# Two block ends, eight feed-forward edges: one norm folded into the next, and VectorE and ScalarE work put in another order

## The chip, the cores and the metric

The kernel runs on one core of a Trainium2 chip. The metric is the device time of one execution in microseconds (us); lower is better. The engines are TensorE (PE in the rows; its weight loads are PEld), VectorE (DVE), ScalarE (ACT), GpSimd (POOL) and SyncE (SP), which issues the weight DMAs.

## The reference

Batch 1, 256 tokens, width 1024, in float32. A first block of two hybrid attention layers ends in an RMS norm; its output is the input of a second block, in which each of two layers is a feed-forward, a mixer (recurrent, then spatial) and a feed-forward again.

```python
def rms_norm(x, w):                      # rms_norm_2 is the same, with NORM_EPS = 1e-6 = EPS
    xf = x.astype(jnp.float32)
    y = xf * lax.rsqrt(jnp.mean(xf * xf, axis=-1, keepdims=True) + EPS)
    return (y * w.astype(jnp.float32)).astype(x.dtype)

def swiglu(x, w_in, w_out):              # w_in: 1024 x 5632, w_out: 2816 x 1024
    g, u = jnp.split(x @ w_in, 2, axis=-1)
    return (jax.nn.silu(g) * u) @ w_out

    x = x + gate_x * merge_branches(...)          # end of a hybrid layer; @ w_out is its last product
...
    return rms_norm(x, final_norm_w)              # end of the first block

    for i in range(DEPTH):                        # second block, DEPTH = 2
        h = h + 0.5 * swiglu(rms_norm_2(h, ffn1_norm[i]), ffn1_w_in[i], ffn1_w_out[i])
        hn = rms_norm_2(h, mix_norm[i])
        h = h + m                                 # m: mixer of hn
        h = h + 0.5 * swiglu(rms_norm_2(h, ffn2_norm[i]), ffn2_w_in[i], ffn2_w_out[i])
    return rms_norm_2(h, final_norm)
```

Between the first block and the second two norms follow each other: with x the output of the last hybrid layer, the feed-forward reads rms_norm_2(rms_norm(x, final_norm_w), ffn1_norm[0]), and the residual goes on from rms_norm(x, final_norm_w).

## The kernel before

**Layout.** Activations lie with the model's 1024 columns on partitions, as 8 chunks (KC) of 128, and tokens along the row: `x[:, k, 0:256]` is chunk k. The weights are 516 tiles of 128x1024 floats. SyncE brings them in order into a ring of 6 (`raw`). Each float32 weight is multiplied as two float32r parts: ScalarE copies a tile to `w_hi` (L1626, ring of 4), VectorE subtracts to get `w_lo` (L1924). Both are the step `split(t)`. Activations are split likewise: `h_hi` by ScalarE (L1642), `h_low` by VectorE (L2019). Here the step is called `split_x`.

**A feed-forward** has FC = 22 hidden chunks i and three weight tiles for each: g (gate), u (up) and o (down), in the order g0 u0 g1 u1 o0 g2 u2 o1 ... g21 u21 o20 o21. A g or u tile is 8 chunk products of two matmuls each (L2490 over 512 columns, `h_hi` and `h_low` side by side, and L2492), an o tile is 8 output chunks of three matmuls (L2482 to L2484). The gate lands in PSUM bank G[i % 2] and the up product in S[i % 2]; the downs gather in four output banks, M among them after the norm is through with it. For each i VectorE sums the two halves of the gate (L2289), multiplies by `rstd` (L2292), ScalarE takes Silu (L1780), GpSimd multiplies by `rstd` again (L1552, for the up half of the product), VectorE sums the up half (L2305) and multiplies (L2308), ScalarE makes `hid_hi` (L1785) and VectorE `hid_lo` (L2313); the down of i needs both. The last chunk's up product is taken in one piece, so it has no sum (L2303 instead of L2305 and L2308). The feed-forward's code on each engine is a hand-written order: two rounds by hand at the start, a loop over four rounds at a time (ROUND), and four rounds and the tail by hand. AHEAD = 3: in round i the splits of the tiles five to seven places on stand between the steps of round i.

**The norm is late.** A feed-forward multiplies un-normed chunks (x times the norm's weight) and puts the root in afterwards, since it is a factor per token. The squares (ScalarE L1636) are added (VectorE L1935) and summed over partitions on TensorE (`norm_mean`, L2598), VectorE adds EPS (L2012), GpSimd takes the power -0.5 (L1517), TensorE spreads it over the partitions (`norm_spread`, L2638) and VectorE copies it to `rstd` (L2004). `norm_mean` stands behind u0 and `norm_spread` within g1, at chunk 5. Before the second block only one norm isn't late: the last hybrid layer's ("residual"), which the next norm's squares need. It stands between the blocks with matmuls on constants to fill the time (`keep_busy`, L2542), and scales x itself (L2056).

**The order.** `build_schedule` makes one list of steps, and each engine runs its part of it in that order; `add_after_split` puts a step behind the next split. `bank_residuals` is the list behind a feed-forward (and behind the recurrent mixer): per output bank a residual (L2356) and the splits of its two chunks, then one weight split and the squares that are left (`late_squares`).

**Waits.** A step waits for counters of other engines. A weight split of tile n on ScalarE waits until TensorE has used tile n - 4; TensorE's first product of a tile waits for its `w_lo`.

## Time and profile before

| | us |
|---|---|
| median of 3 runs | 1994.42 (1992.77 to 1996.35) |
| the profiled execution | 1993.69, of which its span is 1992.0 |
| TensorE busy | 1952.9 (98%) |
| VectorE busy | 1220.5 (61%) |
| ScalarE busy | 894.3 (45%) |
| GpSimd busy | 227.9 (11%) |

The blocks meet at 1038 us. The feed-forwards begin their first tile at about 1044, 1323, 1514 and 1791 us and their last down ends at about 1237, 1514, 1706 and 1979 us. The recurrent mixer lies between the first and the second, the spatial one between the third and the fourth; the third follows the second directly. Matmuls overlap in the pipeline: a row gives a matmul's start and how long it was under way, and what counts for the time is the distance from start to start. Where TensorE waited, a row ends in the idle time in brackets, counted from the end of the matmul before. The idle time is thus less than what the wait cost.

### The profile page before, as it was taken

The numbers are of one execution on the slowest core, as the hardware profiler recorded it, in microseconds if no ns is written. First come the engines' busy times: TensorE is split into PE (matmuls) and PEld (weight loads), VectorE is DVE, ScalarE is ACT, GpSimd is POOL, SyncE is SP. The second block draws the span as 40 slices with busy tenths as digits, with TensorE's granted clock in tenths as the row PEclk, the third lists the DMA queues.
The fourth block names the chain that finished last, engine by engine and source line by source line (L and its number), as shares of the span: only waits on it lengthen the run. The fifth ranks groups of instructions, "written<-read, shape, count | busy, mean of one in ns | idle before, by whom it ended". The sixth has DMA issues, their size and how long they took to land. (4 is left out here: it accounts for less than half of the span.)

```text
span 1992.0 us, 35392 instructions
## 1 busy us (share of the span) xinstructions
PE 1952.9 (98%) x13247; PEld 1703.2 (86%) x13247; DVE 1220.5 (61%) x1962; ACT 894.3 (45%) x1426; POOL 227.9 (11%) x241
## 2 busy tenths in 40 slices
PE   8999999999999999999999999999999999999998
PEld 6777887777787788998998999989998999998997
DVE  6554443355443655546557777887777777676775
ACT  5444232244332544335545444764445444554443
POOL 1000100111122001211121000000001000201000
PEclk9999999999999999999999999999999999999999
DMA  8221443411234323343355555445555555445553
GB/s 317 82 72 64 144 145 128 145 62 58 80 103 151 111 93 104 109 142 114 129 169 166 184 188 170 150 156 184 188 190 183 188 189 188 151 157 172 190 186 109
DMA packets 79429, 289.23 MB, mean 145 GB/s; under 512 B 8912, under 2 KB 9168, under 8 KB 79312
## 3 DMA queue, kind: packets, MB, share of 16 engines
q1 hardware_dynamic: 77616, 281.61, 42.4%
q0 software_dynamic: 1120, 4.72, 0.8%
q8 instruction: 85, 1.39, 0.3%
q10 hardware_dynamic: 576, 1.24, 0.2%
q14 instruction: 32, 0.26, 0.1%
HBM read 286.49 MB, written 1.05 MB: 144 GB/s over the span
## 5 line engine op out<-in xcount | busy, mean ns | idle before, releaser
L1924 DVE TENSOR_TENSOR w_lo<-raw,w_hi 128x1024 fp32r<-128x1024 f32 x484 | 598.5, 1241 | 313.2 <-ACT w_hi L1626 312.3
L1626 ACT ACTIVATE w_hi<-raw 128x1024 fp32r<-128x1024 f32 x484 | 508.0, 1055 | 407.9 <-PE bank L2484 247.6
L2490 PE MATMUL bank<-h,w_hi 128*128 128x512 f32 x1376 | 487.6, 396 | 4.0 <-DVE h L2019 3.4
L2482 PE MATMUL bank<-h,w_hi 128*128 128x512 f32 (+1 forms) x1344 | 473.3, 352 | 3.6 <-issue 1.7
L2484 PE MATMUL bank<-h,w_lo 128*128 128x512 f32 (+1 forms) x1344 | 453.1, 337 | 0.0
L2483 PE MATMUL bank<-h,w_hi 128*128 128x512 f32 (+1 forms) x1344 | 452.2, 336 | 0.0
L2492 PE MATMUL bank<-h,w_lo 128*128 128x256 f32 x1376 | 385.6, 280 | 0.0
L2490 PEld LDWEIGHTS bank<-h,w_hi 128*128 128x128 f32 x1376 | 258.1, 188 | 62.8 <-DVE h L2019 4.5
L2482 PEld LDWEIGHTS bank<-h,w_hi 128*128 128x128 f32 x1344 | 254.2, 189 | 53.8 <-issue 28.2
L2484 PEld LDWEIGHTS bank<-h,w_lo 128*128 128x128 f32 x1344 | 254.2, 189 | 28.3
L2483 PEld LDWEIGHTS bank<-h,w_hi 128*128 128x128 f32 x1344 | 254.7, 190 | 24.5 <-issue 1.9
L2492 PEld LDWEIGHTS bank<-h,w_lo 128*128 128x128 f32 x1376 | 259.9, 189 | 0.0
L2482 PE MATMUL bank<-hid_hi,w_hi 128*128 128x256 f32 x704 | 198.0, 281 | 8.5 <-DVE hid_lo L2313 8.4
L2483 PE MATMUL bank<-hid_lo,w_hi 128*128 128x256 f32 x704 | 197.1, 280 | 0.0
L2484 PE MATMUL bank<-hid_hi,w_lo 128*128 128x256 f32 x704 | 196.9, 280 | 0.0
L2482 PEld LDWEIGHTS bank<-hid_hi,w_hi 128*128 128x128 f32 x704 | 132.3, 188 | 13.7 <-DVE w_lo L1924 6.0
L1552 POOL TENSOR_TENSOR silu_g<-silu_g,rstd 128x256 f32<-128x256 f32 x88 | 65.6, 745 | 631.5 <-ACT silu_g L1780 631.5
L1780 ACT ACTIVATE silu_g<-silu_g 128x256 f32<-128x256 f32 x88 | 36.9, 419 | 215.2 <-DVE silu_g L2292 215.2
L2483 PEld LDWEIGHTS bank<-hid_lo,w_hi 128*128 128x128 f32 x704 | 132.5, 188 | 0.0
L2484 PEld LDWEIGHTS bank<-hid_hi,w_lo 128*128 128x128 f32 x704 | 132.3, 188 | 0.0
L1717 ACT ACTIVATE work<-bank,row_stat 128x512 f32<-128x512 f32 (+1 forms) x96 | 58.4, 613 | 67.8 <-DVE row_stat L2175 67.8
L2175 DVE TENSOR_REDUCE row_stat<-bank 128x1 f32<-128x512 f32 (+1 forms) x96 | 53.0, 593 | 33.8 <-PE bank L2670 33.8
(242 smaller groups left out, 2383.4 us busy)
## 6 DMA issues: line engine op xcount, KB each, us to landing
raw<-in_weights SPq DMA_DIRECT2D x516, 512.0 KB, 3.4
early<-in_first SPq DMA_DIRECT2D x10, 512.0 KB, 13.2
bias<-in_rpb POOLq DMA_DIRECT2D x8, 384.0 KB, 3.4
early_o<-in_first SPq DMA_DIRECT2D x4, 512.0 KB, 16.3
x<-in_tokens SPq DMA_DIRECT2D x2, 512.0 KB, 6.0
x<-in_tokens ACTq DMA_DIRECT2D x2, 512.0 KB, 8.4
work<-in_first SPq DMA_DIRECT2D x2, 512.0 KB, 16.4
out<-cols_out SPq DMA_DIRECT2D x4, 256.0 KB, 2.6
```

What stands on the lines that cost most here:

```text
L1552: pool.tensor_tensor(v, v, rstd[:, 0:SEQ], ALU.mult).then_inc(silu_scaled, 1)
L1626: nc.scalar.activation(w_hi[:, n % SPLIT, :], raw[:, t % RAW, :], ACT.Copy).then_inc(hi_ready, 1)
L1717: nc.scalar.activation(probs[:, hp, 0:u.keys], S[use % 2][:, 0:u.keys], ACT.Exp, bias=row_stat[:, 0, i:i + 1], accum_out=row_stat[:, 1, i: ...
L1780: nc.scalar.activation(silu_g[:, i % 2, :], silu_g[:, i % 2, :], ACT.Silu).then_inc(silu_ready, 1)
L1924: dve.tensor_tensor(w_lo[:, t % RAW, :], raw[:, t % RAW, :], w_hi[:, SPLIT_NO[t] % SPLIT, :].bitcast(F32), ALU.subtract).then_inc(lo_ready, 1)
L2175: dve.tensor_reduce(row_stat[:, 0, i:i + 1], s[:, 0:u.keys], AX_X, ALU.max, negate=True)\
L2482: nc.tensor.matmul(dst, w_hi[:, SPLIT_NO[t] % SPLIT, at], hi, start=start, stop=False, skip_group_check=shared)
L2483: nc.tensor.matmul(dst, w_hi[:, SPLIT_NO[t] % SPLIT, at], lo, start=False, stop=False, skip_group_check=shared)
L2484: return nc.tensor.matmul(dst, w_lo[:, t % RAW, at], hi, start=False, stop=stop, skip_group_check=shared)
L2490: nc.tensor.matmul(bank[:, :], w_hi[:, SPLIT_NO[t] % SPLIT, at], h[:, k, 0:BOTH], start=k == 0, stop=k == KC - 1, skip_group_check=True)
L2492: return nc.tensor.matmul(bank[:, 0:SEQ], w_lo[:, t % RAW, at], h_hi[:, k, 0:SEQ], start=False, stop=k == KC - 1, skip_group_check=True)
```

## The change

**Blocks' end.** The norm between the blocks is no step of its own any more. The last hybrid layer's products go on as before, and behind each of them the chunk is split at once with `fold_w` = final_norm_w * ffn1_norm[0], and squared. TensorE sums squares with two columns, w/D and w*w/D (`fold_cols`), behind the products 3 to 7 of `w_out`, and the last three within the feed-forward's `norm_mean`. From the two means VectorE makes two sums in two dependent operations, GpSimd takes four roots instead of two, `norm_spread` spreads 512 columns instead of 256: the root of both norms together in `rstd[:, 0:256]` and the first norm's own in `rstd[:, 256:512]`. The residual x is scaled by the latter in the first feed-forward's last four rounds (`renorm`, 8 operations on VectorE), and `bank_residual` waits for it. The two steps of filling matmuls (26 in the trace) go.

**Start of each feed-forward.** VectorE sums gate 0, takes the mean, splits tile t0+3, sums up 0, copies `rstd`, scales gate 0, scales up 0 by `rstd` itself and multiplies; then it splits t0+4. GpSimd has no part in chunk 0. In round 0 `hid` and `low` stand ahead of the next split.

**End of each feed-forward.** VectorE's last product and `low` stand ahead of the split a+3. On TensorE five output chunks of o20 stand ahead of o21's instead of four.

**Behind a feed-forward and the recurrent mixer.** The late squares stand ahead of the weight split instead of behind it.

```diff
@@ schedule_layer
+    if layer:
+        s.add("fold_weights")
+        norm = new_norm(s, live, "h", "fold", "fold")
+        jobs = s.product_pair(("w_out", "w_out"), n=live, src="m")
+        for dc in range(KC):
+            job = jobs[dc] if dc < 2 else s.product("w_out", n=live, src="m", norm=None)
+            up = s.add("gated_residual", job=job, dc=dc, layer=layer, cols=live)
+            add = s.add if dc == KC - 1 else s.add_after_split
+            norm.chunks.append(add("split_x", norm=norm, k=dc, up=up, h=s.count("h")))
+            square(s, norm, dc, 1, up, after_split=dc < KC - 1)
+            if dc >= 3:
+                norm_part(s, norm, dc - 3)
+        return norm
@@ build_schedule
-    norm.how, norm.layer = "residual", ("final_norm_w", 0)
-    s.flush()
-    norm_mean(s, norm)
-    s.keep_busy(5, "G")
-    norm_spread(s, norm)
-    s.keep_busy(8, "G")
-    before, norm = norm, new_norm(s, SEQ, "h", ("ffn1_norm", 0), "dve")
-    for q in range(KC // 2):
-        ups = [normed(s, before, k) for k in (2 * q, 2 * q + 1)]
-        follow(s, norm, q, [None] * (2 * q) + ups)
-    late_squares(s, norm)
@@ bank_residuals
+    late_squares(s, after)
     if s.tile < NT:
         s.add("split", t=s.tile + AHEAD - 1)
-    late_squares(s, after)
@@ vector: norm_mean_step, norm_spread_step
+                if norm.add_n == "fold":
+                    dve.wait_ge(m_full, norm.m + 1)
+                    dve.wait_ge(rstd_rows, norm.rows)
+                    means = M[:, 0:4].rearrange("p (b two) -> p two b", two=2)
+                    dve.tensor_scalar(row_mean[:, 2:4], means[:, 0, :], EPS, None, ALU.add).then_inc(fold_mean, 1)
+                    dve.wait_ge(fold_mean, 1)
+                    dve.scalar_tensor_tensor(out=row_mean[:, 0:2], in0=row_mean[:, 2:4], scalar=EPS,
+                                             in1=means[:, 1, :], op0=ALU.mult, op1=ALU.add).then_inc(m_free, 1)
+                    return
...
+                if norm.add_n == "fold":
+                    dve.tensor_copy(rstd[:, :], M[:, :]).then_inc(m_free, 1)
+                    return
@@ vector: renorm, and the steps of the first chunk in ffn_step
+            def renorm(k, norm):
+
+                at = PARAM_AT["final_norm_w"] + k
+                dve.scalar_tensor_tensor(out=x[:, k, 0:SEQ], in0=x[:, k, 0:SEQ], scalar=par[:, at:at + 1],
+                                         in1=rstd[:, SEQ:BOTH], op0=ALU.mult, op1=ALU.mult).then_inc(renormed, 1)
...
+                def first_mult():
+                    dve.wait_ge(up_summed, UP_SUMS * f + 1)
+                    dve.tensor_tensor(hidden[:, 0, :], hidden[:, 0, :], rstd[:, 0:SEQ], ALU.mult).then_inc(up_scaled, 1)
+                    dve.wait_ge(up_scaled, f + 1)
+                    dve.wait_ge(silu_ready, FC * f + 1)
+                    dve.tensor_tensor(hidden[:, 0, :], hidden[:, 0, :], silu_g[:, 0, :], ALU.mult).then_inc(hid_ready, 1)
...
                 def round_(i, r=None):
                     a = t0 + AHEAD + 3 * i
-                    split(a + 2, r)
-                    low(i, r)
+                    if i == 0:
+                        low(0)
+                        split(a + 2)
+                    else:
+                        split(a + 2, r)
+                        low(i, r)
...
                     else:
                         gate(i + 1)
-                        split(a + 3)
                         mult(i + 1)
                         low(i + 1)
+                        split(a + 3)
                         split(a + 4)
 
+                gate_sum(0)
+                norm_mean_step(st)
                 split(t0 + AHEAD)
-                split(t0 + AHEAD + 1)
-                norm_mean_step(st)
+                first_up_sum()
                 norm_spread_step(st)
                 dve.wait_ge(m_free, st.norm.m_spread + 1)
-                gate(0)
-                mult(0)
+                gate_scale(0)
+                first_mult()
+                split(t0 + AHEAD + 1)
                 round_(0)
...
                 for i in range(FC - 1 - peeled, FC - 1):
+                    if st.norm.add_n == "fold":
+                        for k in range(2):
+                            renorm(2 * (i - (FC - 1 - peeled)) + k, st.norm)
                     round_(i)
@@ tensor: last_downs
-                    down(FC - 2, dcs=range(4), done=False)
+                    down(FC - 2, dcs=range(5), done=False)
                     down(FC - 1, dcs=range(4), done=False)
-                    for dc in range(4, KC, 2):
-                        down(FC - 2, dcs=(dc, dc + 1), first=False, done=dc == KC - 2)
-                        down(FC - 1, dcs=(dc, dc + 1), first=False, done=dc == KC - 2)
+                    down(FC - 2, dcs=(5,), first=False, done=False)
+                    down(FC - 1, dcs=(4, 5), first=False, done=False)
+                    down(FC - 2, dcs=(6, 7), first=False)
+                    down(FC - 1, dcs=(6, 7), first=False)
```

How the instructions stand is shown for three places. The first is TensorE where the blocks meet; `m_hi` is the last hybrid layer's input of `w_out`, `h` the feed-forward's. Before:

```order
L2484 MATMUL bank<-m_hi,w_lo 128x256
L2598 MATMUL bank<-con,scaled 128x1 x2
L2598 MATMUL bank<-con,square 128x1 x2
L2542 MATMUL bank<-con 128x128 x5
L2638 MATMUL bank<-con,stats 128x128 x2
L2542 MATMUL bank<-con 128x128 x8
L2490 MATMUL bank<-h,w_hi 128x512
```

After:

```order
L2561 MATMUL bank<-m_lo,w_hi 128x256
L2562 MATMUL bank<-m_hi,w_lo 128x256
L2675 MATMUL bank<-fold_cols,square 128x2 x2
L2568 MATMUL bank<-h,w_hi 128x512
L2570 MATMUL bank<-h,w_lo 128x256
```

Of the mean, the filling matmuls and the spread nothing is left between the blocks but one pair of sums; each such matmul is two records in the trace.

The second is VectorE from the second feed-forward's last chunk to the third's first. Before, from the last gate's scaling on:

```order
L2292 TENSOR_TENSOR silu_g<-silu_g,rstd 128x256
L1924 TENSOR_TENSOR w_lo<-raw,w_hi 128x1024
L2303 TENSOR_TENSOR hidden<-silu_g,bank 128x256
L2313 TENSOR_TENSOR hid_lo<-hidden,hid_hi 128x256
L1924 TENSOR_TENSOR w_lo<-raw,w_hi 128x1024
L2356 SCALAR_TENSOR_TENSOR x<-bank,x 128x2x256 x2
```

After:

```order
L2341 TENSOR_TENSOR silu_g<-silu_g,rstd 128x256
L2352 TENSOR_TENSOR hidden<-silu_g,bank 128x256
L2379 TENSOR_TENSOR hid_lo<-hidden,hid_hi 128x256
L1947 TENSOR_TENSOR w_lo<-raw,w_hi 128x1024 x2
L2433 SCALAR_TENSOR_TENSOR x<-bank,x 128x2x256 x2
```

The last product and its low part stand ahead of both weight splits, and the residuals still stand behind both.

The third is VectorE at the third feed-forward's start, from the last chunks' low parts (`h`) on. Before:

```order
L2019 SCALAR_TENSOR_TENSOR h<-x,par,h 128x256 x4
L1924 TENSOR_TENSOR w_lo<-raw,w_hi 128x1024
L1935 TENSOR_TENSOR scaled<-scaled,square 128x512 x3
L1924 TENSOR_TENSOR w_lo<-raw,w_hi 128x1024 x2
L2012 TENSOR_SCALAR stats<-bank 128x2
L2004 COPY rstd<-bank 128x256
L2289 TENSOR_REDUCE silu_g<-bank 128x256
L2292 TENSOR_TENSOR silu_g<-silu_g,rstd 128x256
L2305 TENSOR_REDUCE hidden<-bank 128x256
L2308 TENSOR_TENSOR hidden<-silu_g,hidden 128x256
L1924 TENSOR_TENSOR w_lo<-raw,w_hi 128x1024
L2313 TENSOR_TENSOR hid_lo<-hidden,hid_hi 128x256
```

After:

```order
L1958 TENSOR_TENSOR scaled<-scaled,square 128x512 x3
L1947 TENSOR_TENSOR w_lo<-raw,w_hi 128x1024
L2335 TENSOR_REDUCE silu_g<-bank 128x256
L2062 TENSOR_SCALAR stats<-bank 128x2
L1947 TENSOR_TENSOR w_lo<-raw,w_hi 128x1024
L2367 TENSOR_REDUCE hidden<-bank 128x256
L2039 COPY rstd<-bank 128x256
L2341 TENSOR_TENSOR silu_g<-silu_g,rstd 128x256
L2371 TENSOR_TENSOR hidden<-hidden,rstd 128x256
L2374 TENSOR_TENSOR hidden<-hidden,silu_g 128x256
L1947 TENSOR_TENSOR w_lo<-raw,w_hi 128x1024
L2379 TENSOR_TENSOR hid_lo<-hidden,hid_hi 128x256
```

Both sums stand ahead of the copy of `rstd`, each weight split has moved by some places, and the product of up 0 and `rstd` is new.

## Rows read from the trace of the kernel before

**Rows 1.** The page's busy times: us, share of the span, instructions.

```profile
PE 1952.9 (98%) x13247; PEld 1703.2 (86%) x13247; DVE 1220.5 (61%) x1962; ACT 894.3 (45%) x1426; POOL 227.9 (11%) x241
```

**Rows 2.** Waits of TensorE: line waited for, total us, times, longest us.

```profile
PE bank L2482 <- DVE hid_lo L2313: 8.4, 7, 1.7
...
PE bank L2638 <- POOL stats L1517: 2.4, 5, 1.1
```

**Rows 3.** Timeline of TensorE at the blocks' meeting: start, us, instruction, idle before.

```profile
1038.00 0.28 PE L2484 MATMUL bank<-m_hi,w_lo 128*128 128x256 f32 x1
...
1043.98 0.47 PE L2490 MATMUL bank<-h,w_hi 128*128 128x512 f32 x1 [0.47 <-DVE h L2019]
...
1053.29 1.02 PE L2598 MATMUL bank<-con,scaled 128*128 128x1 f32 x8
1054.16 0.48 PE L2490 MATMUL bank<-h,w_hi 128*128 128x512 f32 x1
...
1056.32 0.71 PE L2638 MATMUL bank<-con,stats 128*128 128x128 f32 x4 [0.16 <-POOL stats L1517]
...
1056.79 0.48 PE L2490 MATMUL bank<-h,w_hi 128*128 128x512 f32 x1
...
1062.10 0.36 PE L2482 MATMUL bank<-hid_hi,w_hi 128*128 128x256 f32 x1 [1.18 <-DVE hid_lo L2313]
```

**Rows 4.** Timeline of the fourth feed-forward's first chunk, all engines.

```profile
1799.70 0.42 DVE L2004 COPY rstd<-bank 128x256 f32<-128x256 f32 x1 [2.13 <-PE bank L2638]
...
1801.91 0.75 POOL L1552 TENSOR_TENSOR silu_g<-silu_g,rstd 128x256 f32<-128x256 f32 x1 [3.56 <-ACT silu_g L1780]
...
1802.69 0.43 DVE L2308 TENSOR_TENSOR hidden<-silu_g,hidden 128x256 f32<-128x256 f32 x1 [0.78 <-POOL silu_g L1552]
...
1803.03 1.22 DVE L1924 TENSOR_TENSOR w_lo<-raw,w_hi 128x1024 fp32r<-128x1024 f32 x1
...
1804.17 0.42 DVE L2313 TENSOR_TENSOR hid_lo<-hidden,hid_hi 128x256 fp32r<-128x256 f32 x1
...
1804.73 0.36 PE L2482 MATMUL bank<-hid_hi,w_hi 128*128 128x256 f32 x1 [1.25 <-DVE hid_lo L2313]
```

**Rows 5.** Timeline of the first feed-forward's end, TensorE and VectorE.

```profile
1230.56 1.23 DVE L1924 TENSOR_TENSOR w_lo<-raw,w_hi 128x1024 fp32r<-128x1024 f32 x1 [1.44 <-ACT w_hi L1626]
...
1230.63 0.28 PE L2482 MATMUL bank<-hid_hi,w_hi 128*128 128x256 f32 x1
...
1231.70 0.41 DVE L2303 TENSOR_TENSOR hidden<-silu_g,bank 128x256 f32<-128x256 f32 x1
...
1233.17 0.36 PE L2482 MATMUL bank<-hid_hi,w_hi 128*128 128x256 f32 x1 [0.96 <-DVE hid_lo L2313]
...
1234.69 1.28 DVE L2356 SCALAR_TENSOR_TENSOR x<-bank,x 128x512 f32<-128x512 f32 x2
...
1236.02 0.89 DVE L2019 SCALAR_TENSOR_TENSOR h<-x,par,h 128x256 fp32r<-128x256 f32 x2
...
1237.52 0.28 PE L2482 MATMUL bank<-h,w_hi 128*128 128x256 f32 x1
```

**Rows 6.** Timeline of TensorE at the third feed-forward's start.

```profile
1521.29 1.02 PE L2598 MATMUL bank<-con,scaled 128*128 128x1 f32 x8 [0.42 <-DVE scaled L1935]
...
1524.54 0.71 PE L2638 MATMUL bank<-con,stats 128*128 128x128 f32 x4 [0.36 <-POOL stats L1517]
```

**Rows 7.** Timeline of a round in the second feed-forward's loop.

```profile
1361.20 0.42 DVE L2313 TENSOR_TENSOR hid_lo<-hidden,hid_hi 128x256 fp32r<-128x256 f32 x1
...
1364.05 0.40 PE L2490 MATMUL bank<-h,w_hi 128*128 128x512 f32 x1
...
1364.40 0.28 PE L2482 MATMUL bank<-hid_hi,w_hi 128*128 128x256 f32 x1
```

**Rows 8.** Timeline of VectorE at the third feed-forward's end.

```profile
1698.77 1.96 DVE L1924 TENSOR_TENSOR w_lo<-raw,w_hi 128x1024 fp32r<-128x1024 f32 x1 [1.43 <-ACT w_hi L1626]
```

**Rows 9.** A stretch of the recurrent mixer: busy us by engine, TensorE's granted clock, DMA.

```profile
1306.00:1308.00 2.00, 2.00 (x11) 2.00 (x11) 2.00 (x4) 1.05 (x2) 0.00 (x0) 0.50 0.03 8
```

More of the change, by code:

```diff
@@ L748, in square @@
     i = len(norm.units)
-    summed = i > 0 and (norm.add_n == "dve" and chunks == 2 or norm.add_n != "pe" and not last)
+    on_pe = norm.add_n in ("pe", "fold")
+    summed = i > 0 and (norm.add_n == "dve" and chunks == 2 or not on_pe and not last)
     st = add("square", norm=norm, k=k, blocks=chunks, up=up, first=i == 0, last=last, slot=i % 2,
-             before=norm.units[i - 2] if i >= 3 and norm.add_n != "pe" else None, outs=None,
+             before=norm.units[i - 2] if i >= 3 and not on_pe else None, outs=None,
              add_n=s.count("sq_add") if summed else None)
@@ L885, in schedule_ffn @@
 def schedule_ffn(s, norm, how, weight, adds):
-    norm.m, norm.rows = s.use("M"), s.count("rows")
+    if norm.part is None:
+        norm.m = s.use("M")
+    norm.rows = s.count("rows")
     norm.m_spread = s.use("M")
@@ L2594, in sums @@
                 c = norm.cols
+                if norm.add_n == "fold":
+                    for b in range(c // P):
+                        ins = nc.tensor.matmul(M[:, 2 * b:2 * b + 2], square_of(u)[:, P * b:P * b + P],
+                                               fold_cols[:, u.k, :], start=start and b == 0, stop=stop,
+                                               skip_group_check=True)
+                    return ins
                 for j in range(norm.units[0].blocks):
@@ L2616, in norm_mean @@
                     pe.wait_ge(m_free, norm.m)
-                if norm.part is not None:
+                if norm.add_n == "fold":
+                    units = norm.units[-3:]
+                elif norm.part is not None:
                     units = norm.units[-1:]
```

66 lines of the change are left out of this document (50 added, 16 removed).

## The prediction

> **What bounds the kernel now.** I read the page first: TensorE is busy for 98% of the span [rows 1], so time is won only where TensorE stands still, or where it does work of its own that can go. Next the waits of TensorE over the whole span [rows 2]: the largest entry is the down product waiting for `hid_lo`, 8.4 us in 7 waits, which are the starts of all four feed-forwards and the ends of three. The spread's wait for GpSimd's roots follows with 2.4 us in 5. The timeline where the blocks meet shows what that list can't: filling matmuls count as work [rows 3]. A wait costs more than its bracket: idle time is counted from the end of a matmul (0.28 under way, 0.12 from start to start), so 0.16 is lost besides, and the first matmul behind it takes 0.08 longer. Each wait that goes is worth its bracket plus 0.24.
>
> **Pitches.** A pair of a g or u tile takes 0.35 us from start to start [rows 7]. An output chunk of a down (three matmuls) takes 0.355: 12 of them, with the start after a wait, take 4.35 [rows 5]. Eight records of `norm_mean` take 0.87 and make the next matmul 0.08 longer [rows 3]: 0.12 each. Four of `norm_spread` take 0.47 and 0.08 [rows 3], so eight take 1.0.
>
> **A, the blocks' meeting.** Before, from 1038.12 (0.12 behind the last `w_out` matmul) to the first down at 1062.10 it is 24.0 us [rows 3]. What has to stay are four tiles, 32 x 0.35 = 11.2. The change adds to TensorE's stream five pairs of sums of four records (two matmuls are four records, as in the rows before), 20 x 0.12 = 2.4, three pairs in `norm_mean`, 12 x 0.12 = 1.4, and a spread of eight records, 1.0. Together 16.0. The chunk work that was in series (roots, spread, copy, scaling x, splits) now stands behind each `w_out` product: VectorE has per product a residual and a low part of 0.45 each and a `w_lo` of 1.23 [rows 5], 2.1 us of 2.85 (24 x 0.12); ScalarE has one weight copy and two operations on a chunk, less than that. Chunk 7 is ready some 1.8 us behind the last product; tile g0 asks for it after 0.5 of sums and 7 x 0.35. The bank of g0 isn't the last `w_out` product's, so it needn't wait for that residual. The second sum of the means and its semaphore aren't in the trace; bounds are nothing (it hides in the five pairs between mean and spread, 1.75 us, of which sum and root fill 1.1 elsewhere) and 0.5, I take nothing. The copy of 512 columns is bounded by the copy of 256, 0.42 [rows 4], and two residuals of 512 columns in 1.28 [rows 5]; I take 0.7. With it `hid_lo` of chunk 0 comes 4.95 us behind the start of the spread, and TensorE arrives after 1.0 + 11 x 0.35 = 4.85, so 0.2 is left of the wait of 1.18. A gives 24.0 - 16.2 = **7.8**, between 6.3 and 8.3. GpSimd's memset and DMA issues for the mixer's gates now start earlier, behind chunk 7, and are over before the roots are asked for. The 8 scalings of x, 0.48 each, lie in four rounds in which VectorE has about 2 us to spare: nothing.
>
> **B, the other starts.** Take the fourth [rows 4]. Now: copy 1799.70, sum, scale, Silu, GpSimd 0.75 (till 1802.66), product 1802.69, a weight split, `hid_lo` till 1804.59, TensorE 1804.73. In the new order both sums are done before the copy: scale till 1800.6, Silu and the new product beside each other till 1801.05, product till 1801.5, split of t0+4 till 1802.7, `hid_lo` till 1803.1. TensorE is free at 1804.73 - 1.25 - 0.16 = 1803.3. The wait goes: 1.25 + 0.24 = 1.5. What is late next is that weight split, with 0.2 in hand. The split of t0+3, now behind the mean, ends 1.7 ahead of u1. The second and third have two waits more, since the late squares no longer stand behind a split: at the third the sums wait 0.42 and the spread 0.36 [rows 6], with 0.24 each 1.3. The price is that g1's `w_lo` moves behind the squares: they begin one weight copy on ScalarE (about 1 us) earlier than before, so that at the third the last sum ends near 1520.1 (before 1521.2) and `w_lo` near 1521.4, and TensorE, through with the mean 0.95 behind 1521.29 - 0.42 - 0.16 = 1520.7, asks for it at 1521.6. That is close: 0 to 0.3 each. I take 2.5 for each of the two. B gives 2.5 + 2.5 + 1.5 = **6.5**, between 4.5 and 7.2.
>
> **C, the ends.** At the first [rows 5] the last product stands behind a weight split until 1231.70, though its bank is full at 1230.8, 0.16 behind the start of the downs at 1230.63, and its gate before that. Ahead of the split, `hid_lo` ends at 1232.2, and with five chunks for cover TensorE arrives at 1230.63 + 5 x 0.355 = 1232.4: no wait. The downs then end at 1230.63 + 16 x 0.355 = 1236.3 instead of 1237.52. But the residuals still stand behind both splits and begin at 1234.6 instead of 1234.69, and chunk 0's low part [rows 5] can't be there before 1236.4. So 1.0 of 1.2. At the second end the next consumer is g0, a chunk every 0.35, while VectorE needs 4 x 0.64 + 8 x 0.445 = 6.1 us for the 8 chunks [rows 5]: g0's end is tied to VectorE, which starts only 0.1 earlier. 0.15. At the third the wait is the longest, 1.7 [rows 2], since the split ahead of the product took 1.96 instead of 1.23 [rows 8], beside GpSimd's masking of `ws`. Now the product itself stands beside that masking. If it is slowed as much as the split was, 0.7, the end gives 1.0, if not 1.7. I take 1.4. The fourth has no split and gives 0.1. C gives **2.65**, between 0.5 and 3.4.
>
> A page bears on that third end. The Trainium skill, "GPSIMD Engine Reference", Specifications, has GpSimd's SBUF interfaces shared with VectorE, with contention for VectorE instructions that have two SBUF inputs. The split reads two, the product one (the other is in PSUM). By the page the product isn't slowed and the total is 17.2, by the row's stretch 16.5; the trace agrees for the split.
>
> **Sum.** 7.8 + 6.5 + 2.65 = 17.0 us. Against the profiled execution, 1993.7 (1.7 of it outside the span), that is 1976.7; the median of the three runs lies 0.7 above that execution, so the forecast is **1977.4**.
>
> **Rivals.**
> 1. The recurrent mixer takes back what the first end gives. For: in its second half VectorE is busy all the time, TensorE stands still for it and then runs at half clock (0.50 granted, 1.2 GHz) [rows 9]. A TensorE that comes 1.0 earlier may only wait 1.0 longer. Against: in its first half VectorE waits for TensorE. The same may befall the third end: 1.0 + 1.4 less, **1979.8**.
> 2. The first chunk's wait doesn't go, since a weight split still stands between product and `hid_lo`, and each start keeps about 1 us: **1981.4**. For: only 0.2 in hand. Against: GpSimd's 0.75 and a sum of 0.69 are gone for certain.
> 3. The folded work holds up `w_out`, so that the change doesn't do what it says there: VectorE has 0.7 to spare per product and the low part stands behind a split that waits for ScalarE. If each of seven products is held up by 0.7: 4.9 less, **1982.3**. Against: four tiles are split ahead.
> 4. The clock. Once the fillers are gone a wait at the blocks' meeting could make TensorE fall to 1.2 GHz as in the mixer [rows 9], where eleven matmuls took 2 us instead of 1.3. In the mean and spread of the new order no wait is left that long; a fall would cost about 1.5: **1978.9**. The Trainium skill, "TensorE: Matmul & The Clock Gate", Part 1, has the clock follow how busy TensorE was of late; by that rule the missing fillers speak against the change only if a wait takes their place.
> 5. Slower. In the loop `hid_lo` is ready at 1361.62 and used at 1364.40 [rows 7], 2.8 in hand. TensorE now enters the rounds about 2.7 earlier against VectorE. If VectorE did not gain on it, each of 84 rounds would wait. From 0.2 us per round this outweighs the 17 us; at 0.3 it is 25: **2002**. Against: VectorE's work in a round (three splits, two sums, three products, about 6.3 us) leaves 2 of 8.4 to catch up with.
>
> **How the numbers follow.** Forecast 0.62, rival 1 0.13, rival 2 0.12, rival 3 0.05, rival 4 0.05, rival 5 0.03. With the lower bounds of A, B and C (11.3) it would be 1983.1, with the upper ones (18.9) 1975.5; a mixer stall that goes as well would take 3 more. The range 1973.0 to 1982.5 holds the forecast and rivals 1, 2 and 4, and leaves out rival 5 and most of 3. A measurement tells 0.2% (4 us) from no change: faster by more 0.95, within 0.02 (rivals 2 and 3 at their worst together), slower 0.03.
>
> **What would show it.** Right: from the last `w_out` matmul to the first down about 16.2 us with no filler; no TensorE wait for `hid_lo` above 0.3; the third feed-forward's mean and spread without a wait; the first downs' end near 1.0 earlier against its tile. Wrong: a new TensorE wait for `w_lo` of g1 or of o0, for h at the mixers' start above 0.5, a stall in the recurrent mixer above 2.4, or GpSimd's roots late behind the four-column power.

## The result, and the profile after

The changed kernel takes 1982.43 us (median of 4 runs, 1981.85 to 1984.97), the kernel before 1994.57 (median of 4, 1992.77 to 1996.35): a ratio of 0.9941, with a 95% interval of 0.9929 to 0.9953. That is 12.1 us, where 17.0 were forecast (1977.4, range to 1982.5). Faster was right; 5 us of the gain did not arrive.

The profiled execution has a span of 1980.1 us, 11.9 less than before. Its busy times answer to [rows 1]:

```profile
PE 1952.4 (99%) x13237; PEld 1705.6 (86%) x13237; DVE 1217.8 (62%) x1965; ACT 891.7 (45%) x1422; POOL 218.0 (11%) x230
```

TensorE's share went from 98 to 99%, and yet its busy time is the same as before, 1952.4 us against 1952.9, although fillers were taken out. So what had been waits has gone, and something else grew. The waits of TensorE (engine, line, releaser: us in total, times, longest), to be read against [rows 2]:

```profile
PE bank L2726 <- POOL stats L1535: 3.2, 6, 1.1
PE bank L2560 <- DVE w_lo L1947: 3.2, 3, 2.3
```

The entry for `hid_lo`, 8.4 us before, doesn't exist any more. The one for GpSimd's roots grew from 2.4 to 3.2. TensorE's timeline at the blocks' meeting (start, duration, operation, in brackets the idle time before it), against [rows 3]:

```profile
1035.71 0.51 PE L2675 MATMUL bank<-fold_cols,square 128*128 128x2 f32 x4
...
1036.08 0.48 PE L2568 MATMUL bank<-h,w_hi 128*128 128x512 f32 x1
...
1042.17 1.03 PE L2675 MATMUL bank<-fold_cols,scaled 128*128 128x2 f32 x8
...
1045.68 0.71 PE L2726 MATMUL bank<-con,stats 128*128 128x128 f32 x4 [0.62 <-POOL stats L1535]
...
1050.62 0.35 PE L2560 MATMUL bank<-hid_hi,w_hi 128*128 128x256 f32 x1
```

No filler stands there now, g0 starts behind the last sums, and the spread waits 0.62 for GpSimd. The last of these rows, 1050.62, is the start of `down(0)`. The next two rows are the start of `down(20)`, 20 rounds later, and of the mixer's first matmul, behind the last downs. Before, the three stood at 1062.10 [rows 3], 1230.63 and 1237.52 [rows 5].

```profile
1221.27 0.28 PE L2560 MATMUL bank<-hid_hi,w_hi 128*128 128x256 f32 x1
...
1227.03 0.32 PE L2560 MATMUL bank<-h,w_hi 128*128 128x256 f32 x1
```

The end takes 5.76 us instead of 6.9. But the 20 rounds between take 170.65 us, where they took 168.5: 8.53 a round instead of 8.43, in a stretch in which neither kernel's TensorE waits. Two windows of 100 us in the first feed-forward's loop, before and then after (busy us and number of records of TensorE's matmuls and weight loads, VectorE, ScalarE, GpSimd; granted clock, DMA share, GB/s), say the same:

```profile
1100.00:1200.00 100.00, 100.00 (x668) 91.71 (x667) 71.13 (x96) 44.51 (x60) 8.95 (x12) 1.00 0.57 189
```
```profile
1100.00:1200.00 100.00, 100.00 (x661) 91.41 (x660) 71.50 (x98) 44.61 (x60) 8.92 (x12) 1.00 0.55 184
```

TensorE is busy all the time at a granted clock of 1.00, and does 661 matmuls instead of 668. The whole difference, cut at marks that both timelines have (us, each from the starts of two matmuls; `oa_hi` is the first product of an attention output in the last hybrid layer, at 1012.15 before and 1007.71 after):

| stretch | before | after | gain | forecast |
|---|---|---|---|---|
| start of the program to the first layer's products | 53.1 | 51.7 | 1.4 | 0 |
| first layer and second hybrid, to `oa_hi` | 959.0 | 956.0 | 3.1 | 0 |
| from `oa_hi` over the blocks' meeting to the first down (A) | 49.95 | 42.9 | 7.0 | 7.8 |
| 4 x 20 rounds | 674.2 | 682.4 | -8.2 | 0 |
| first end | 6.9 | 5.8 | 1.1 | 1.0 |
| recurrent mixer and second start | 101.5 | 99.4 | 2.0 | 2.5 |
| second end and third start | 22.8 | 20.4 | 2.4 | 2.65 |
| third end | 7.6 | 5.8 | 1.8 | 1.4 |
| spatial mixer and fourth start | 98.3 | 97.7 | 0.6 | 1.5 |
| fourth end to the last spread | 10.75 | 10.5 | 0.3 | 0.1 |

The rows from the meeting to the last spread, without the rounds, come to 15.3 us together. What is missing is the pace of the rounds, which takes 8.2, less 3.1 won by a faster pace in a layer that the change doesn't touch.

The row of the blocks' meeting depends on the execution for the kernel before. In this profile of it TensorE's granted clock was 1.00 throughout the meeting; in a second one of the same kernel (`b_again`) it was 0.50 from 1050 to 1053 us, among the same waits for `h` (0.5, 0.9, 0.9 and 0.9 us). First this profile, then the second:

```profile
1050.00:1053.00 3.00, 3.00 (x19) 2.59 (x18) 1.96 (x4) 2.71 (x5) 2.63 (x3) 1.00 0.38 126
```
```profile
1050.00:1053.00 3.00, 3.00 (x11) 2.61 (x10) 2.06 (x4) 2.70 (x5) 2.70 (x3) 0.50 0.23 72
```

TensorE does 11 matmuls there instead of 19, and the row of the table is 50.97 instead of 49.95. The two other variants of the kernel before that are profiled below, `b_shift` and `b_pads`, have the half clock there too, with 51.8 and 51.2. None of the 14 profiles with the folded norm has it; all of them have 1.00 from 1030 to 1056 us. From g0's first matmul to the first down it is 18.1 us without it and 19.1, 19.7 and 19.1 with it, so the half clock costs 1.0 to 1.6 us, which the fold saves as well in three of the four profiles of the old meeting. How often the clock falls there in executions without a profile isn't known.

### The profile page after: what moved, and what is told of

It reads as the page before. It is cut to its first block and busy times, and to the rows that moved or that the text cites. A ratio compares the mean times of both kernels' runs of the same rounds, so it can differ in the third digit from the quotient of the medians.

```text
span 1980.1 us, 35364 instructions
## 1 busy us (share of the span) xinstructions
PE 1952.4 (99%) x13237; PEld 1705.6 (86%) x13237; DVE 1217.8 (62%) x1965; ACT 891.7 (45%) x1422; POOL 218.0 (11%) x230
## 5 line engine op out<-in xcount | busy, mean ns | idle before, releaser
L2221 DVE TENSOR_REDUCE row_stat<-bank 128x1 f32<-128x512 f32 (+1 forms) x96 | 53.1, 594 | 33.7 <-PE bank L2758 33.7
```

Of the source, the lines that this page charges most:

```text
L2221: dve.tensor_reduce(row_stat[:, 0, i:i + 1], s[:, 0:u.keys], AX_X, ALU.max, negate=True)\
```

## Experiment 1: is the pace the execution's, the program's or the place's?

The changed kernel allocates two small tiles, `fold_w` and `fold_cols`, in front of `stats`: 96 bytes a partition, by which `square`, `rstd`, `scaled`, the hybrids' buffers, `silu_g`, `hidden`, `hid_hi`, `hid_lo` and the mixers' buffers move on (`x`, `w_hi`, `w_lo`, `raw` and `h` lie in front and stay). The theory: where an operand lies in SBUF sets how fast TensorE's matmuls follow each other. The rivals: the changed instructions do it, or it differs from execution to execution. Four runs; `b_again` and `a_again` are the two kernels once more.

> The kernel before, unchanged, a second profiled execution. In the first profile a round of a feed-forward lasts 8.417 us and the downs' matmuls follow each other every 0.1177 us; in the changed kernel 8.527 and 0.1200, with no wait in either. Theory P (the pace belongs to the program, by where its buffers lie or how its instructions lie): again 8.417, within 0.01, and the first layer reaches its first product with m_hi near 604 us less what the start's transfers differ. Theory E (the pace belongs to the execution): another value, anywhere between 8.41 and 8.53.

> The kernel before with the two small tiles of the change (96 bytes a partition) allocated in front of stats, used by nobody: all buffers behind them (square, rstd, scaled, the hybrid's, silu_g, hidden, hid_hi, hid_lo, the mixers') lie 96 bytes further on, as in the changed kernel; no instruction differs otherwise. Theory A (addresses set the pace): rounds of 8.527 us instead of 8.417, 84 x 0.11 = 9.2 us lost, less some 3.3 won in the first 650 us: slower by 5 to 6 us, near 2000. Theory I (the changed instructions set it) and theory E (the execution): as the kernel before, 1994.6, ratio 1.000.

```diff
         neg_half = sb("neg_half", [P, 1])
+        fold_w = sb("fold_w", [P, KC])
+        fold_cols = sb("fold_cols", [P, KC, 2])
         stats = sb("stats", [P, 2, 8])
```

> The changed kernel with its two small tiles allocated behind all others, so that every other buffer lies where it lay before the change. Theory A: rounds of 8.42 us again, 8 us won in the feed-forwards, 3.3 lost in the first 650 us: near 1977.5, which is what the prediction's sum gives. Theories I and E: as the changed kernel, 1982.4.

```diff
-        fold_w = sb("fold_w", [P, KC])
-        fold_cols = sb("fold_cols", [P, KC, 2])
         stats = sb("stats", [P, 2, 8])
...
         ws_b = sb("ws_b", [P, KC, P], stack=mixer)
         mixer.close()
+        fold_w = sb("fold_w", [P, KC])
+        fold_cols = sb("fold_cols", [P, KC, 2])
```

> The changed kernel, unchanged, on the same chip as the two others, for the comparison. All theories but E: 1982.4, rounds of 8.527 us. Theory E: rounds of another length.

| kernel | us (median, lowest to highest) | ratio to before (95%) | 4 x 20 rounds | first layer and second hybrid |
|---|---|---|---|---|
| before, same chip | 1993.67 (1992.46 to 1996.09) | | 674.2 | 959.0 |
| b_again | 1994.56 (one) | | 674.15 | 959.1 |
| b_shift | 2001.60 (2000.41 to 2002.06) | 1.0038 (1.0024 to 1.0052) | 682.6 | 956.3 |
| a_again | 1983.06 (1981.42 to 1983.86) | 0.9946 (0.9930 to 0.9963) | 682.4 | 955.7 |
| a_end | 1976.71 (1976.55 to 1977.01) | 0.9913 (0.9896 to 0.9930) | 674.0 | 959.4 |

(The last two columns are of the profiled executions, the last one up to `oa_hi`; those of before are the first profile's.) The pace doesn't belong to the execution: both repeats agree with their first within 0.1 us in 674. It doesn't belong to the instructions: two tiles that nobody uses make the kernel before 8 us slower in the rounds and 3 faster in the first layer, and the changed kernel with its tiles elsewhere has the old rounds. In all, b_shift lost 7.9 us where 5 to 6 were expected; in its profile some 1.6 of them are the half clock at the meeting. The window of a_end in the loop, at the same granted clock as above, has 669 matmuls, one more than before:

```profile
1100.00:1200.00 100.00, 100.00 (x669) 91.71 (x668) 71.54 (x98) 44.70 (x60) 8.90 (x12) 1.00 0.55 189
```

At the old places the change gives 1993.67 - 1976.71 = 17.0 us, at the new ones 2001.60 - 1983.06 = 18.5. The timelines give, from the first layer's products on, 15.4 at the old places with the first profile of before and 16.5 with b_again, and 18.9 at the new ones; the meeting is 7.3, 8.3 and 8.9 of it.

## Experiment 2: GpSimd's roots, and which buffer sets the pace

The spread's waits at the second and third start, forecast to go, are still there, and the roots are the longest thing before them. The roots of two columns at the second start, on GpSimd, in the kernel before:

```profile
1332.47 0.70 POOL L1517 TENSOR_TENSOR stats<-stats,neg_half 128x2 f32<-128x2 f32 x1 [83.73 <-DVE stats L2012]
```

and in a_end, with what VectorE does from then on:

```profile
1321.72 0.15 DVE L2062 TENSOR_SCALAR stats<-bank 128x2 f32<-128x2 f32 x1
1321.78 1.22 DVE L1947 TENSOR_TENSOR w_lo<-raw,w_hi 128x1024 fp32r<-128x1024 f32 x1
```
```profile
1321.95 1.61 POOL L1535 TENSOR_TENSOR stats<-stats,neg_half 128x2 f32<-128x2 f32 x1 [82.36 <-DVE stats L2062]
```

0.70 us before, when VectorE had nothing to do behind the mean; 1.61 now, beside a weight split that began 0.17 earlier and ends at 1323.0: the root ends 0.56 behind it. The four-column root at the meeting takes 1.94, where four columns take 1.02 elsewhere. The trace of the kernel before had such roots already, outside the feed-forwards' starts: this one, of the mixer's norm, began 0.23 behind the first of two splits.

```profile
1246.97 2.35 DVE L1924 TENSOR_TENSOR w_lo<-raw,w_hi 128x1024 fp32r<-128x1024 f32 x2
```
```profile
1247.20 1.54 POOL L1517 TENSOR_TENSOR stats<-stats,neg_half 128x2 f32<-128x2 f32 x1 [16.80 <-DVE stats L2012]
```

> a_end (the changed kernel with its small tiles behind all others), and in the start of every feed-forward VectorE takes the sum of tile u0 between the mean and the first weight split, so that GpSimd's roots run beside a reduction out of PSUM instead of beside a split with two SBUF inputs. Theory L (GpSimd's root stands still while VectorE's split runs: it takes 1.61 us instead of 0.70 in the second, third and fourth feed-forward, 1.94 instead of 1.02 for four columns at the blocks' meeting): the roots take 0.70 and 1.02, the spread's waits of 0.3 to 0.6 us at the four starts go, 0.24 more each: about 2 to 2.8 us less than a_end, 1974.3. Theory N (the longer root has another cause, such as the larger start-up of GpSimd after its DMA issues): roots as long as before, the same 1976.7, or a little more since a split comes 0.7 later.

```diff
                 norm_mean_step(st)
-                split(t0 + AHEAD)
                 first_up_sum()
+                split(t0 + AHEAD)
```

a_root: 1975.30 us (1973.33 to 1976.36), ratio 0.9899 (0.9882 to 0.9915). The roots of the four starts take 1.03, 0.70, 0.72 and 0.69. The second start, VectorE and GpSimd:

```profile
1321.56 0.68 DVE L2367 TENSOR_REDUCE hidden<-bank 128x256 f32<-128x512 f32 x1
1322.16 1.22 DVE L1947 TENSOR_TENSOR w_lo<-raw,w_hi 128x1024 fp32r<-128x1024 f32 x1
```
```profile
1321.72 0.70 POOL L1535 TENSOR_TENSOR stats<-stats,neg_half 128x2 f32<-128x2 f32 x1 [82.25 <-DVE stats L2062]
```

Beside a reduction out of PSUM the root takes as long as alone (0.70), beside a split that reads two buffers of SBUF and began ahead of it 1.61. A split that begins behind the root's start leaves it as it is: here it begins 0.44 behind, and in the kernel before one begins 0.10 behind the root at 1739.08, which takes 0.70 too. The waits for the roots fell from 3.2 us in 6 to 1.9 in 3. From the first layer's products on, a_root's timeline is 3.05 us shorter than a_end's (its start of the program was 1.0 longer, as starts differ from execution to execution). The medians differ by 1.4, from two chips; against the kernel before on the same chip the gain is 19.6 instead of 17.0, 2.6 more, with intervals of about 3 us to either side. Theory L holds by the roots' durations and the waits; its 2 to 2.8 us lie within what the three measures leave. The Trainium skill, "SBUF — State Buffer", Who interferes with whom, has VectorE and GpSimd arbitrate for a pair of ports as an exclusive lock, where the second one waits until the first is through; the rows agree in kind: the root that began second ends 0.56 behind the split's end, a little less than the 0.70 that it takes alone. The other way round they don't show it: the split that began 0.10 behind the root of 1739.08 takes 1.22 as ever.

> The changed kernel (small tiles in front of stats, 96 bytes), and 32 unused bytes in front of silu_g: the first layer's buffers, rstd and square lie as in the changed kernel, all buffers of the feed-forwards and mixers lie at 128 bytes from their old place. Theory A1 (the pace of the rounds hangs on the address modulo 64 of the feed-forward's own buffers): rounds of 8.42 us and the first layer's faster pace, 3.3 us better than a_end: 1973.4. Theory A2 (it hangs on rstd, square or scaled): rounds of 8.527, 1982.4.

> The changed kernel, and 32 unused bytes between hidden and hid_hi: silu_g and hidden lie as in the changed kernel, hid_hi and hid_lo (the two that TensorE reads in the downs) and the mixers' buffers at 128 bytes from their old place. Theory A1a (TensorE's own operand counts): rounds of 8.42 us, the downs' matmuls 0.1177 apart, near 1973.5. Theory A1b (the buffers of the other engines count, silu_g and hidden): rounds of 8.527, near 1982.4. If both count, something between.

> The changed kernel, and 116 unused bytes in front of stats: square, rstd, scaled, the hybrids' buffers, silu_g, hidden, hid_hi and hid_lo all begin at a multiple of 256 bytes. Theory A with aligned reads best: both the first layer and the rounds run faster than in any kernel so far, rounds under 8.42 us and below 1973. If only the place within 64 bytes counts and 0 is like 12: as the changed kernel, rounds of 8.527, 1982.4.

The edits are one line each, in front of `silu_g` (shown), of `hid_hi` and, with 29 columns instead of 8, of `stats`:

```diff
+        pad = sb("pad", [P, 8])
         silu_g = sb("silu_g", [P, 2, SEQ])
```

The places are bytes, counted from the sizes in the order of allocation; the kernel before has `hid_hi` at 44, the changed one at 140.

| kernel | us | hid_hi and hid_lo, modulo 256 | rstd, modulo 256 | 4 x 20 rounds |
|---|---|---|---|---|
| a_mix | 1971.70 (1971.02 to 1973.19), ratio 0.9884 (0.9868 to 0.9901) | 172 | 140 | 671.0 |
| a_hid | 1973.63 (one) | 172 | 140 | 671.1 |
| a_zero | 1982.27 (one) | 0 | 0 | 680.1 |

A1 and A1a hold: moving `hid_hi` and `hid_lo` alone (a_hid leaves `silu_g` and `hidden` where the changed kernel has them) does all that a_mix does. That the place modulo 64 decides falls: 44 and 172 are alike modulo 64, and give 674.0 and 671.0. And a_zero, with everything at a multiple of 256 bytes, is nearly as slow as the changed kernel. The Trainium skill, "SBUF — State Buffer", Specifications, has SBUF made of lines of 16 bytes, with a price for each crossing to a new one. One might infer that a buffer at a multiple of 16 does best; these runs don't show it: all places but a_zero's are at 12 modulo 16, and they are both faster and slower.

## Experiment 3: the parts of the change alone, and the pace by address

> a_end (the changed kernel at the old addresses) with the ends of the feed-forwards as before the change: VectorE's last product and low part behind the split of t0+3, and the last downs in the old order. By the prediction's term C it is 2.65 us slower than a_end, near 1979.4. By the traces of before and a_end set side by side (1.1 + 1.3 + 2.0 + 0.5 at the four ends) it is up to 4.9 slower, near 1981.6; less, if part of what the second end shows belongs to the start behind it.

> a_end with the ends as before and the starts as before too: both splits, then mean and spread, GpSimd scaling the first activation, VectorE's and ScalarE's round 0 in the old order, the late squares behind the split. Only the folded norm at the blocks' meeting is left of the change. By term A it is 7.8 us faster than before, 6.3 to 8.3; here the first feed-forward's start has its wait for hid_lo back as well (1.4), so about 6.4: near 1988. Rivals: if the fold was the smaller part, above 1990; with all of the gain in the fold, near 1978.

| kernel | us (median, lowest to highest) | ratio to before (95%) |
|---|---|---|
| before, same chip | 1994.89 (1994.64 to 1996.16) | |
| no_bc (the fold alone) | 1987.09 (1986.20 to 1987.91) | 0.9958 (0.9941 to 0.9975) |
| no_c (fold and starts) | 1981.08 (1980.54 to 1983.22) | 0.9933 (0.9916 to 0.9949) |
| a_end (all) | 1976.71 (1976.55 to 1977.01) | 0.9913 (0.9896 to 0.9930), other chip |

no_c puts the old order of the ends back, in VectorE's last round and in `last_downs`:

```diff
                         gate(i + 1)
+                        split(a + 3)
                         mult(i + 1)
                         low(i + 1)
-                        split(a + 3)
                         split(a + 4)
...
-                    down(FC - 2, dcs=range(5), done=False)
+                    down(FC - 2, dcs=range(4), done=False)
...
```

no_bc does so too, and puts back the old starts:

```diff
-                gate_sum(0)
-                norm_mean_step(st)
                 split(t0 + AHEAD)
-                first_up_sum()
+                split(t0 + AHEAD + 1)
+                norm_mean_step(st)
                 norm_spread_step(st)
                 dve.wait_ge(m_free, st.norm.m_spread + 1)
-                gate_scale(0)
-                first_mult()
-                split(t0 + AHEAD + 1)
+                gate(0)
+                mult(0)
                 round_(0)
```

with GpSimd's `scale_silu(0)`, the order of round 0 and the late squares as before. By the medians the fold gives 7.8 us, the starts 6.0 and the ends 4.4. The ends are across two chips; by the two ratios it is 4.0, and each ratio's interval is about 3 us to either side, so the times alone don't tell the ends from nothing. The timelines, which are free of the start of the program, give 6.7 for the fold against the first profile of before and 7.7 against b_again (no_bc has 43.28 from `oa_hi` to the first down). They give for the starts 0.6 at the first feed-forward, 2.1, 2.1 and 1.2 at the others, and for the ends 1.1, 0.3, 1.9 and 0, together 3.3. At the second end 1.2 us are won until g0 and 0.9 of them are gone at the mean: VectorE's residuals and chunks decide there, as the prediction had it.

> a_end with hid_hi and hid_lo of the four feed-forwards laid 0, 32, 64 and 96 bytes behind their old place (44, 76, 108 and 140 modulo 256); every other buffer stays. Theory H (the place of hid_hi and hid_lo against the other buffers sets the pace of TensorE's matmuls, in steps): the first feed-forward has rounds of 8.41 us, and the others other lengths, between 8.38 and 8.53. If only 32 bytes of difference count (modulo 64), first and third are alike, second and fourth alike. If the pace hangs on something else, all four have 8.41.

> The same with 128, 160, 192 and 224 bytes (172, 204, 236 and 12 modulo 256). Theory H with a period of 64 bytes: 8.41 or 8.38 in the first and third, another value in the second and fourth. With a period of 128 bytes: the four of scan1 again in the same order.

```diff
-        hid_hi = sb("hid_hi", [P, 2, SEQ], F32R)
-        hid_lo = sb("hid_lo", [P, 2, SEQ], F32R)
+        hid = sb("hid", [P, 4 * SEQ + 64], F32R)
+        hid_parts = [[hid[:, at + j * BOTH:at + j * BOTH + BOTH].rearrange("p (b t) -> p b t", b=2) for j in range(2)]
+                     for at in (0, 8, 16, 24)]
...
```

The three places that write or read the two buffers take the pair of their feed-forward.

In scan1 the first feed-forward's `down(0)` and `down(20)` stand at 1055.45 and 1223.97; those of the second, with 32 bytes, and the fourth, with 96:

```profile
1329.46 0.28 PE L2561 MATMUL bank<-hid,w_hi 128*128 128x256 f32 x1
...
1495.25 0.29 PE L2561 MATMUL bank<-hid,w_hi 128*128 128x256 f32 x1
...
1786.50 0.28 PE L2561 MATMUL bank<-hid,w_hi 128*128 128x256 f32 x1
...
1957.08 0.28 PE L2561 MATMUL bank<-hid,w_hi 128*128 128x256 f32 x1
```

165.8 us for the same 20 rounds in the second, 170.6 in the fourth. With scan3, of Experiment 4, all places of `hid_hi` and `hid_lo` (bytes behind the old place; us a round over 20 rounds):

| 0 | 16 | 32 | 48 | 64 | 96 | 128 | 160 | 192 | 224 | 288 | 544 |
|---|---|---|---|---|---|---|---|---|---|---|---|
| 8.43 | 8.51 | 8.29 | 8.41 | 8.39 | 8.53 | 8.39 | 8.43 | 8.44 | 8.50 | 8.29 | 8.29 |

scan1 took 1977.09 us and scan2 1980.65 (one run each). Theory H holds, and the period isn't 64 (32 and 96 differ) or 128 (32 and 160 differ).

## Experiment 4: both kernels at chosen places

> a_root (old addresses, VectorE's sum of u0 ahead of its first split) with 96 unused bytes in front of the hybrids' buffers and 32 in front of hid_hi. Theory H (each group of matmuls has the pace of its own operand's place, and it adds up): the first 650 us 3.3 us shorter as in the changed kernel, rounds of 8.279 us as in scan1's second feed-forward instead of 8.414, 84 x 0.135 = 11.3: 1975.3 - 14.6, near 1961. If the gain in scan1's second feed-forward hung on the others lying elsewhere: rounds near 8.41 and 1972.

> The kernel before with the same two pads. Theory H: the same 14.6 us as there, near 1980, which would be less than the changed kernel as it is (1982.4), without one instruction moved. If the pace were a matter of the changed order as well: less of it, 1985 to 1995.

```diff
+        hb("pad_front", [P, 24])
         outs = ExitStack()
         early_o = hb("early_o", [P, 4, D], stack=outs)
...
+        sb("pad_hid", [P, 8])
         hid_hi = sb("hid_hi", [P, 2, SEQ], F32R)
```

> a_pads with 32 unused bytes in front of the hybrids' buffers instead of 96 (76 modulo 256, the place where hid_hi is fastest). If one place is best for all operands: the first layer's products with m_hi under 0.2275 apart (0.2342 at the old place, 0.2275 at 140), and 1 to 4 us less than a_pads. If it hangs on more than the operand's own place: another value, unknown sign.

> a_end with hid_hi and hid_lo of the four feed-forwards 288, 16, 48 and 544 bytes behind their old place. With a period of 256 bytes the first has rounds of 8.28 us, as 32 bytes gave, with a period of 512 only the fourth (or neither, with a longer one). The second and third show the step: if it is 32 bytes, 16 is like 0 or 32 (8.414 or 8.279), and 48 like 32 or 64 (8.279 or 8.383).

| kernel | us (median, lowest to highest) | ratio to before (95%) | 4 x 20 rounds | first layer and second hybrid |
|---|---|---|---|---|
| before, same chip | 1994.27 (1992.25 to 1997.97) | | 674.2 | 959.0 |
| b_pads | 1980.59 (1979.03 to 1982.97) | 0.9933 (0.9916 to 0.9949) | 663.6 | 956.0 |
| a_pads | 1960.63 (1958.88 to 1962.62) | 0.9829 (0.9812 to 0.9845) | 663.2 | 956.1 |
| a_pads2 | 1964.05 (one) | | 663.15 | 958.4 |

The window of a_pads in the first feed-forward's loop, 677 records where before had 668 and after 661:

```profile
1100.00:1200.00 100.00, 100.00 (x677) 91.94 (x677) 73.13 (x100) 46.17 (x61) 8.89 (x12) 1.00 0.54 189
```

The effects of the two pads add up: 13.7 us for the kernel before, 14.7 for a_root (from two chips), where 14.6 were expected. That each group of matmuls goes by its own operands' place alone isn't shown, and in the rounds it isn't so (see what is left open). 128 unused bytes alone make the kernel before as fast as the changed one is as it stands. a_pads beats both, by 33.6 and 21.8 us. a_pads2, which had the hybrids' buffers at 32 too, was to be 1 to 4 us faster if one place were best for all, and is 3.4 slower. Up to `oa_hi` 96 bytes are 2.3 us better than 32, while for `hid_hi` 32 are better than 96. From `oa_hi` to the first down it is 32 that is better, by 1.0 (40.9 against 41.9), with the same buffers `m_hi` and `m_lo` read in 256 columns instead of 512. So no one place is good for all. scan3 (1975.01, one run) shows that the pace of 32 comes back at 288 and 544, as a period of 256 bytes gives, and that 16 bytes already change it. No other place was measured 256 bytes on.

## Why the prediction missed

- **The step that failed** is the one under "Pitches": 0.35 for a pair of a g or u tile and 0.355 for a chunk of a down were read from the kernel before and held for the kernel after. They aren't set by the shapes alone: in the rounds the downs' matmuls are 0.1176 apart before and 0.1200 after (pitches from start to start). 4 x 20 rounds cost 8.2 us more and the first layer 3.1 less, for 96 bytes in the allocation. The two lines that allocate the tiles were costed at nothing by not being costed at all, and nothing in the range stood for them. That the time still came so near the range's upper end owes 3.1 us to the first layer, which is luck.
- **A, the blocks' meeting**: 7.0 by the timeline (7.3 in a_end), 7.8 by no_bc's median, which still has the old start, against a forecast of 7.8 with the new one. The sign "about 16.2 us" from the last `w_out` matmul reads 14.9, since four of the five pairs of sums stand ahead of that matmul; with 4 x 0.45 for them it is 16.7, or 0.5 over. The short term is GpSimd's roots, 1.94 us instead of 1.0, hence 0.62 of wait at the spread and its 0.24; the wait for `hid_lo` went whole, where 0.2 was left in the sum. The text named the root as what would show it wrong, but had it late by its four columns (0.3 more), when most of it is the split beside it (0.9). What the sum couldn't see is the half clock of the old meeting, which its one profile doesn't have: against b_again A is 8.1. Rival 4 asked whether the new order would fall to it; it is the old order that did, three times in four.
- **B, the other starts**: forecast 6.5, measured 5.4 (2.1, 2.1, 1.2, from no_bc to no_c; the last stretch alone varies from 97.9 to 98.6 in five profiles of the old start). The waits for `hid_lo` and the mean went, the spread's did not: 0.33 at the second and 0.36 at the third, as long as before, since the root's 0.9 more took the place of the late mean; with 0.24 each that is 1.2, about the difference. The mean ahead of the splits, made for the spread's sake, set the split beside the root. The stretch that the prediction saw at the third end, of a split beside GpSimd's work, bore on this place, and wasn't asked there.
- **C, the ends**: forecast 2.65, by the timelines 3.3 and by the medians 4.4. The first is 1.1 (1.0), the second 0.3 (0.15), the third 1.9 (1.4): the product out of PSUM took 0.42 us beside GpSimd's masking (a_end: from 1685.47, the masking from 1684.98 to 1686.07), as at the first end before (0.41). That was the case that would have given 1.7, so the sum should have taken the other end of that term.
- **Costed at nothing**: the 8 scalings of x are nothing, the first feed-forward's 20 rounds in a_end are 168.57, the others 168.46. The second sum of the means, 0.2 us on VectorE, lies in the root's wait.
- **The rivals**: the mixer takes next to nothing back (101.5 to 99.4 with the start behind it, its stall 2.34 instead of 2.40; from no_c to a_end, where only the ends differ, the stretch grows by 0.15). Behind that stall the granted clock is 0.50 in before [rows 9], 1.00 in after and 0.50 again in a_end, whose stretch is 0.3 longer than after's. Further, the first chunk's wait went everywhere; in the products of `w_out` there is no wait; the granted clock from 1036 to 1050 us is 1.00. Rival 5 said that each of the rounds could become longer, at 25 us for 0.3 a round, by which the 0.1 found makes 8; but it meant a wait, and there is none.

With the same places the change is worth 17.0 to 18.5 us by the medians, where the sum over its mechanisms had 17.0; the time was off by the rounds. That close an agreement is partly luck: by the timeline that the sum was read from, its three parts bring 15.3 (A 7.0, the rest 8.3) instead of 17.0, and the medians hold in addition whatever the old meeting lost to the half clock, 1.0 to 1.6 us where it was seen. That this makes up the difference is argued, not shown.

Left open: why the clock fell in three profiles of the old meeting and not in the fourth, behind the same waits; why the place sets the pace, whether `hid_hi`, `hid_lo` or their distance from the weights counts, and why matmuls that read `h` and `w_hi` also change their pitch in the rounds when only `hid_hi` and `hid_lo` move (0.2304 in before, 0.2330 in after and 0.2278 in a_hid, the mean of the first half of a pair). None of the 16 kernels moved the weights.

## What to carry to other kernels

Before the instructions of two versions are compared, compare where their buffers lie: a small tile allocated in the middle moves all behind it, and here that alone made a round of matmuls 1.3% longer (8.43 to 8.53 us), while over all places tried it spans 3% (8.29 to 8.53). Allocate new small tiles last, and try a few pads in front of TensorE's operands, each group for itself, once the order is settled. And when VectorE is given something to do while another engine's result is awaited, look in the trace for what that result takes beside such an instruction: two instructions exchanged brought GpSimd's roots back from 1.6 to 0.7 us. And look at the granted clock in more than one profile before a stretch with waits is taken as its price.

## What the runs showed of the hardware

- The pitch of fp32r matmuls at a granted clock of 1.00 changes with the SBUF place of their operands (`hid_hi` and `hid_lo`, and the hybrids' buffers): 12 places of `hid_hi` and `hid_lo` gave rounds between 8.29 and 8.53 us, the same at 32, 288 and 544 bytes and differing already at 16. With all these buffers at multiples of 256 (a_zero) a round is among the slow ones (8.50).
- GpSimd's root of two columns takes 0.69 to 0.72 us beside an idle VectorE or its reduction out of PSUM, and 1.53 to 1.63 when a weight split with two inputs in SBUF began ahead of it; of four columns 1.02 and 1.94. A split that began 0.10 us behind the root left it at 0.70.
- Among waits of 0.5 to 0.9 us TensorE's granted clock fell to 0.50 (1.2 GHz) in three profiles of the old meeting, at a cost of 1.0 to 1.6 us, and stayed at 1.00 in one.
- The start of the program, up to the first layer's products, took from 51.3 to 54.7 us in the profiles of these kernels, without a change there.
